# The context mixer's convolution beside the x tokens' second routing pass

## The reference

```python
p  = modulate(rms_norm(h, norm1_g), ...) @ w_in          # q, k, v, pool input, conv input, two conv gates, 3 gates
o  = diff_attn_core(q, k, v, lam)                        # 8 heads, two softmaxes per head
pool = pool_branch(p[pool input], pool_w, pool_scale)
conv = (b_gate * depthwise_conv(c_gate * conv_in, conv_w)) @ conv_out_w      # kernel of 3 tokens
h  = h + gate * ((g0 * attn + g1 * pool + g2 * conv) @ w_out)
# peer_ffn: for each token and 8 heads the best 16 of 128 x 128 experts
s  = einsum(xn2 @ w_q, sub_keys); s1, i1 = top_k(s[0], 16); s2, i2 = top_k(s[1], 16)
top_s, pos = top_k(s1 + s2, 16); eidx = i1 * 128 + i2 at pos; gate = softmax(top_s)
h  = h + m5 * sum_k gate_k * gelu(xn2 . u_emb[eidx_k]) * v_emb[eidx_k]       # 8 x 16 = 128 experts per token
```

## Time and profile before

| | us |
|---|---|
| Time, median of 3 runs (4295.15 to 4298.55) | 4296.83 |
| The profiled execution | 4289.55 |
| Its span | 4287.3 |
| PE busy | 3734.7 (87%) |
| DVE busy | 2834.8 (66%) |
| ACT busy | 1158.1 (27%) |
| POOL busy | 907.4 (21%) |

### The profile page before, as it was taken

How to read it: one execution, slowest core, us unless ns; L and a number is a source line. 1 busy time by engine, 2 the same in 40 slices (tenths; PEclk the granted TensorE clock), 3 DMA queues, 4 the chain that set the end, 5 groups by cost and what they waited for, 6 DMA issues and landing times.

```text
span 4287.3 us, 42560 instructions
## 1 busy us (share of the span) xinstructions
PE 3734.7 (87%) x15389; PEld 2387.8 (56%) x15389; DVE 2834.8 (66%) x6600; ACT 1158.1 (27%) x2577; POOL 907.4 (21%) x772
## 2 busy tenths in 40 slices
PE   7999998788999879987777888777779989999898
PEld 3457554334745535543333554222239879898797
DVE  3241137988877797888785568886656676565764
ACT  2140011124111112122101422111124444444443
POOL 0000013433333343334341024443320000000000
PEclk9999999999999999998898999999999999999999
DMA  6363458988999999999995179999974534455343
GB/s 251 147 256 128 171 195 353 412 346 303 412 420 367 393 394 371 409 378 365 408 421 230 40 313 388 421 383 421 422 306 171 185 129 167 177 176 180 129 167 133
DMA packets 246622, 1225.90 MB, mean 286 GB/s; under 512 B 19256, under 2 KB 46202, under 8 KB 124428
## 3 DMA queue, kind: packets, MB, share of 16 engines
q0 software_dynamic: 110592, 805.36, 46.1%
q1 hardware_dynamic: 135820, 417.84, 26.3%
HBM read 1222.07 MB, written 1.05 MB: 285 GB/s over the span
## 4 chain that ended last, share of the span: by engine, by line
PE 40%; DMA 16%; DVE 15%; ACT 3%; issue 2%; POOL 1%; DVEq 0%; ACTq 0%; SPq 0%; POOLq 0%
PE ps L446 11%; DMA BIG<-in_t_uv,idx 10%; PE ps L795 7%; PE ps L820 7%; PE ps L821 7%; PE ps L822 7%; DMA gbuf<-in_t_uv,idx 4%; DVE BIG L1954 2%; DVE gbuf L1954 2%; DMA wbuf<-in_t_uv,idx 1%; DVE BIG L1947 1%; DVE wbuf L1954 1%; PE ps L434 1%; DVE plo L1995 1%; PE ps L439 1%
## 5 line engine op out<-in xcount | busy, mean ns | idle before, releaser
L446 PE MATMUL ps<-wbuf,BIG 128*128 128x512 f32 x1856 | 824.0, 600 | 7.8 <-ACT BIG L1231 4.4
L2809 POOL DMA_INDIRECT gbuf<-in_t_uv,idx x286 | 336.8, 1178 | 1439.8 <-DVE BIG L1867 835.1
L446 PEld LDWEIGHTS ps<-wbuf,BIG 128*128 128x128 f32 x1856 | 356.0, 193 | 453.9 <-issue 443.9
L1995 DVE TENSOR_TENSOR plo<-wbuf,phi 128x1024 fp32r<-128x1024 f32 (+1 forms) x344 | 401.6, 1180 | 284.5 <-ACT phi L1336 283.8
L795 PE MATMUL ps<-gbuf,BIG 128*128 128x512 f32 x868 | 430.6, 635 | 149.1 <-ACT BIG L1301 149.1
L795 PE MATMUL ps<-BIG 128*128 128x512 f32 x904 | 436.0, 622 | 114.5 <-ACT BIG L1301 114.4
L1316 ACT ACTIVATE BIG<-BIG 128x2 f32<-128x2 f32 x384 | 78.2, 204 | 1445.4 <-DVE BIG L1961 1431.5
L820 PE MATMUL ps<-XH,phi 128*128 128x256 f32 x1472 | 421.6, 286 | 24.6 <-DVE XL L2005 20.7
L1954 DVE CUSTOM_DVE_ANT_0 BIG<-BIG 128x1024 f32<-128x1024 f32 x292 | 355.7, 1221 | 115.6 <-DMA BIG<-in_t_uv,idx 114.8
L1954 DVE CUSTOM_DVE_ANT_0 gbuf<-gbuf,BIG 128x1024 f32<-128x1024 f32 x286 | 348.0, 1221 | 124.3 <-DMA gbuf<-in_t_uv,idx 123.3
L2809 POOL DMA_INDIRECT BIG<-in_t_uv,idx x292 | 342.6, 1173 | 403.3 <-PE ps L795 325.4
(11 more groups left out here) (368 smaller groups left out, 5062.0 us busy)
## 6 DMA issues: line engine op xcount, KB each, us to landing
wbuf<-in_t_in SPq DMA_DIRECT2D x84, 1024.0 KB
wbuf<-in_ffn_wg SPq DMA_DIRECT2D x20, 2048.0 KB, 7.6
wbuf<-in_ffn_wu SPq DMA_DIRECT2D x20, 2048.0 KB, 7.7
wbuf<-in_t_conv SPq DMA_DIRECT2D x48, 768.0 KB
wbuf<-in_t_w_mod SPq DMA_DIRECT2D x32, 1024.0 KB
wbuf<-in_ffn_wd SPq DMA_DIRECT2D x16, 2048.0 KB, 7.9
wbuf<-in_t_peer_wq SPq DMA_DIRECT2D x24, 1024.0 KB
wbuf<-in_w_in SPq DMA_DIRECT2D x14, 1536.0 KB, 6.5
```

Of the source, the lines that this page charges most:

```text
L446: ins = p(mm)(bank, l, r, start=(k == 0), stop=(k == 7))
L1995: v(tt)(lo, W2.of(key, rows_, n)[:, k0:k1, c0:c1], hi.bitcast(F32), ALU.subtract).then_inc(dve_piece.up(q), 1)
L2809: g(nc.gpsimd.indirect_dma_start)(slot, None, I["t_uv"], bass.IndirectOffsetOnAxis(ap=idx[:, tb % 3, j:j + 1], axis=0)).then_inc(g_landed[ ...
```

## The change

The convolution of the context moves from behind the pooled input to beside the routing pass of A 1, on PE, ACT and DVE. The pass goes at 0.5, the convolution at 0.55 with a rate of 0.66, and the remainder of `beside` at 0.72 instead of 0.6. The convolution uses the scratch ring `side_b` (BIG 10240 to 12287) instead of `side4`, and DVE resets that ring on PE's last scores of the pass. SP issues the convolution's tiles ahead of the Q/K tiles. `QT` and `UU` of `beside` move to BIG 18432 (the scores region `SS`), `CV` to BIG 0 (the normalised x tokens, gather buffer 6). So buffer 7 stays with the gathers. ACT's wait for it goes, and SP waits for its last row ahead of layer 1's small rows. The ring has seven buffers up to slot 151, eight for 152 to 219, nine for 220 to 239, then as before. In group A 1 PE adds the v rows of slots 0 to 23 too, and DVE begins its own sum at slot 25.

```diff
-        beside.QT, beside.MM, beside.UU, beside.PL, beside.CV = by_col(24576), by_tok(8192, 2), by_tok(24576, 2), by_col(10240), by_col(24576)
+        beside.QT, beside.MM, beside.UU, beside.PL, beside.CV = by_col(18432), by_tok(8192, 2), by_tok(18432, 2), by_col(10240), by_col(0)
...
-                if n < 2 and T in "BC":
-                    rows_gone(a, {"B": 7, "C": 8}[T])
+                if n < 2 and T == "C":
+                    rows_gone(a, 8)
...
-                        if i == 1:
+                        if i == (25 if T == "A" else 1):
                             v(ts)(ACCB, row, wv[:, i:i + 1], None, ALU.mult).then_inc(dve_exp.up(T, tb, "v", i), 1)
...
-            return (T, tb) not in SHARED or j % 4 == 0 or (T == "A" and j >= 104)
+            return (T, tb) not in SHARED or j % 4 == 0 or (T == "A" and (j < 24 or j >= 104))
...
         def dve_context(v):
             yield from dve_rest(v, "A", 0)
-            yield from scaled(dve_route_pass(v, "A", 0, 1), 0.72, 1)
-            yield from scaled(dve_beside(v), 0.6, 1)
+            route = scaled(dve_route_pass(v, "A", 0, 1), 0.5, 1)
+            yield next(route)
+            yield from alongside(route, scaled(dve_beside_first(v), 0.55, 1), 0.66)
+            yield from scaled(dve_beside(v), 0.72, 1)
             yield 6
             yield from scaled(dve_route_pass(v, "B", 0, 2, 0, 2), 0.6, 1)
+
+        def dve_beside_first(v):
+            v.wait_ge(*pe_peer.at("A", "pq", 3, 3))
+            side_b.reset((pe_route, ("A", 1, 12)))
+            yield from dve_conv(v, "B", 0, beside, side_b)
...
             yield from dve_pooled(v, "B", 0, L)
-            yield from dve_conv(v, "B", 0, L, side4)
             yield from dve_gates(v, "B", 0, L, side4)
...
-                if s == 64:
-                    gat.held, gat.freed[6] = {8, 9}, ((pe_peer, ("A", "pq", 3, 3)),)
-                if s == 90:
-                    gat.held = {7, 8, 9}
-                if s == 140:
-                    gat.held, gat.freed[8] = {7, 9}, ((pe_att, ("B", 3, NH - 1, "s", 1)),)
+                if s == 152:
+                    gat.held, gat.freed[8] = {6, 9}, ((pe_att, ("B", 3, NH - 1, "s", 1)),)
+                if s == 220:
+                    gat.held, gat.freed[6] = {9}, ((pe_mix, ("B", "br", 1, 2, 1)),)
+                if s == 240:
+                    gat.held = {7, 9}
...
+            sync_conv(s, "B", 0)
             sync_qkv(s, "B", 0, 0, range(2))
             sync_pooled(s, "B", 0)
-            sync_conv(s, "B", 0)
...
             after_edge(s, "ahead")
+            rows_gone(s, 7)
             sync_layer_rows(s, 1, sideb.slots[0][:, 0:256])
```

More of the change, by code:

```diff
@@ L2505, in pe_context, with pe_beside_first @@
             yield from pe_rest(p, "A", first.XT)
-            yield from scaled(pe_route_scores(p, "A", "A", 1), 0.72, 1)
-            yield from scaled(pe_beside(p), 0.6, 1)
+            route = scaled(pe_route_scores(p, "A", "A", 1), 0.5, 1)
+            yield next(route)
+            yield from alongside(route, scaled(pe_beside_first(p), 0.55, 1), 0.66)
+            yield from scaled(pe_beside(p), 0.72, 1)
             yield 6
             yield from scaled(pe_route_scores(p, "B", "A", 2, 0, 2), 0.6, 1)
+        def pe_beside_first(p):
+            yield from pe_conv(p, "B", 0, beside)
         def pe_beside(p):
@@ L2518, in pe_beside @@
             yield from pe_pooled(p, "B", 0, L)
-            yield from pe_conv(p, "B", 0, L)
             yield from pe_gates(p, "B", 0, L)
@@ L2610, in act_context, with act_beside_first @@
             yield from act_rest(a, "A")
-            yield from scaled(act_route_pass(a, "A", 1, route_before("A", 1, 0)), 0.72, 1)
-            yield from scaled(act_beside(a), 0.6, 1)
+            route = scaled(act_route_pass(a, "A", 1, route_before("A", 1, 0)), 0.5, 1)
+            yield next(route)
+            yield from alongside(route, scaled(act_beside_first(a), 0.55, 1), 0.66)
+            yield from scaled(act_beside(a), 0.72, 1)
             yield 6
             yield from scaled(act_route_pass(a, "B", 2, route_before("B", 2, 0), 0, 2), 0.6, 1)
+        def act_beside_first(a):
+            yield from act_conv(a, "B", 0, beside, side_b)
         def act_beside(a):
@@ L2623, in act_beside @@
             yield from act_pooled(a, "B", 0, L)
-            yield from act_conv(a, "B", 0, L, side4)
             yield from act_gates(a, "B", 0, L, side4)
```

## The result

| | us |
|---|---|
| Before, median of 20 runs | 4297.34 |
| Changed, median of 20 runs | 4303.77 |
| Forecast | 4283 (4264 to 4300) |
| Ratio, changed to before | 1.0014 (1.0007 to 1.0020) |
| Profiled execution, changed | 4302.12 (span 4300.3) |

What follows compares the result with a forecast made beforehand. The prediction saw no single bound: PE short of work, then DMA, then both full. Terms 203 + 180 + 139 + 55 + 64 + 69 = 710 against 724.0 before, 14 us less: 4296.83 - 14 = 4283, range 4264 to 4300.

Steps and rivals of the forecast that it cites:

- Gates and mixer's end: Two stretches after the pooled input: gates 139 us (before 133.0), mixer's end, norm and rows 55 (before 51.5).
- Pass: A1's routing pass with the convolution beside it: PE binds, 203 us, where the two stretches took 250.0 before.
- My analogue, B's second pass: Same weave with the other convolution, all v rows on PE: 219.8 us, 217.7 busy, 2.1 idle.
- The second rival: In the pass, gathers with seven buffers arrive late while tiles load: pass 233 us, in all 740, +16; chance 0.11.
- Attention and pooled input: Stretch from Q/K products through pooled input: 180 us, bounds 174 and 188, with 9 us idle; before 161.1.
- the first rival: PE's extra 18 rows eat the gain, attention keeps 14 us idle: 725, +1 us; chance 0.27 with the middle cases.
- the prediction's own sign of being wrong: PE idle as before in attention (or above 10 us in the pass behind diagonals while DVE waits for gathers).
- Queries: The context's query stretch after the mixer's end: one more v row on PE, 64 us; DMA 57.
- B's first scores: Last stretch, to the end of A1's experts: one more slot at full DMA, 69 us for 66.3.
- The third rival: Better than forecast: attention without idle (174), gates bound by PE (134), pass 200: 693, -31; chance 0.12, part of faster.
- The edits at nothing: Priced at nothing: buffer counts, buffer 7's wait moved to SP, DVE's queue order, ACT's extra work, SP's tile order.
- The Trainium skill's rule: Each DMA engine takes queues in turn, packet by packet, so a tile under way takes half the rate from gathers.

Runs made afterwards that it cites:

- e3: Changed kernel, but SP loads only an eighth of each of the context's gate, conv-out, w_out and query tiles; 4287.86 us, ratio to before 0.9978.
- e10: Changed kernel with fewer slots beside mixer's end, norm and rows (0.4 for 0.72), more beside gates (0.76) and queries (0.9); 4309.32 us, ratio to before 1.0029.
- e12: Changed kernel with gates, mixer's end, norm and rows at 0.6, queries 0.72, Q/K, attention and pooled input 0.853; 4296.13 us, ratio to before 1.0002.
- e5: Changed kernel with one gather buffer fewer (six) from slot 48 to 151; 4338.32 us, ratio to before 1.0084.
- e9: Changed kernel, but SP loads only a sixth of each tile of the context's convolution; 4298.10 us, ratio to before 1.0005.
- e1: Changed kernel with the old sharing of A1's v rows (every fourth on PE below slot 104); 4310.21 us, ratio to before 1.0033.
- e8: Changed kernel with A1's first 24 v rows half on PE (even slots), half on DVE; 4305.33 us, ratio to before 1.0011.
- e7: Changed kernel with the rest of the context's mixer at 0.6 as before, leftover slots at the weave's end; 4330.99 us, ratio to before 1.0072.

## Why the prediction was wrong

The sum was 710 and became 731.6, so 21.6 us were missing, from four terms.

- **Gates and mixer's end**: 139 + 55 = 194 forecast, 203.6 measured, 9.6 of the 21.6. The failed step is "rows can be gathered up to three slots earlier, in the stretch ahead that has room". The room was there and stayed unused: in the pooled input, ahead of the gates, the DMA share was 0.85, and POOL stood four times for 28.7 us in all until a v row on PE freed a buffer. The gates came out even shorter than said (137), with 4.0 us of PE idle, and the rows owed were paid where PE next needs DVE's queue. So the second failed term is the 7.6 us of chain in the mixer's end, carried over from before, which became 18.5. e3, e10 and e12 show that the two stretches together hang on the rows and slots in the gates: lighter tiles, more slots and fewer slots there change their sum by -11.4, +1.5 and -18.1 us. I also gave the gates five more rows where my own table of slots has six (31 to 37; POOL's count is 32 and 38), 2.5 us of DMA time.
- **Pass**: 203 forecast, 208.3 measured. The mechanism held: PE full (202.2 busy), 24 products spread over it, DMA 0.97. The 199.9 us of work was 2.3 short, and idle was 6 instead of 3, of it one wait of 4.5 us for a diagonal. My analogue, B's second pass, had an eighth buffer for half its length, and e5 shows that buffers count here. The second rival (233 us, tiles starve the gathers) did not come: e9 bounds the tiles at 3 us.
- **Attention and pooled input**: 180 forecast, 184.3 measured. Busy was 171.6 for 171.0 said. Idle was 12.8 instead of 9: the chain stayed nearly as long as before (14.1), as the first rival had it and as the prediction's own sign of being wrong says. That its 18 rows eat the gain was half right. They are 30.9 us of PE's work, but with them on DVE (e1) or half on DVE (e8) the two stretches took 187.8 and 185.2 us.
- **Queries** 63.9 for 64, and **B's first scores** 71.6 for 69: nothing, and 2.6 us. In the scores all of PE's 21.1 us of waiting is for diagonals (L1301); in e1, e3, e5, e8 and e9, with the same slots left for it, the stretch took 67.2 to 70.6 us, so 2.6 us may be this one execution's.

B's first scores start at 1434.3 us, where 1415 was forecast. The mistake behind the first term is that I priced each stretch as the larger of PE's and the DMA engines' need, and let what exceeded it vanish where one stretch ends and the next begins. Of the rivals, the first (+1 us, no change) was nearest: its gates of 145 and end of 56 come to 201, for 203.6 measured. That is luck in part, as its gates were 8 us too long and its end 10.6 too short. The measured change lies within the 0.2% that the prediction gave 0.27. The third rival's sum, 693, takes attention at 171, PE's bare work; with the 174 that it names it is 696. The edits at nothing held: SP issues layer 1's small rows 4.2 us before the end of A1's experts in both kernels (at 1493.47 and 1501.68 us), so its new wait for buffer 7 cost nothing.

The Trainium skill's rule (DMA: Bandwidth & Descriptors, section Queues, rings and completion order), that queues share an engine packet by packet, is neither borne out nor refuted. No run here separates it from a shared total.

## What to carry to other kernels

When work is moved to fill an engine's idle time, also price what takes the place it left: here 20 slots came out of two stretches at 2.1 us each (41.8 us) and went into others at 2.5 us (49.5). Where an engine runs ahead because nothing makes it wait, a debt of the DMA engines isn't gone; look for the next instruction that needs the waiting engine's queue, and put the debt there. Slots moved into a stretch that ends in such a handover are dear, and a scale for each stretch (e12) took the loss away here, though it brought no gain.

## What the runs showed of the hardware

- After PE's wait of 4.76 us at the handover the granted clock was 0.50 to 0.52 for 12 us, in which PE waited another 5.15 us (eight transpose records took 1.94 us for 1.06, sixteen of the products 9.24 for 7.03). After the 2.91 us of waiting ahead of it, eight records still took 1.06.
- The 47 slots of e7's last stretch, most with nothing beside them, took 2.7 us each at a DMA share of 0.95, as those of the routing pass before did (58 slots in 154.2 us). The granted clock averaged 0.71 there, with PE busy 66 of 127.5 us.
- A wait that the profile puts down to "issue" can be another engine's queue: PE's 5.15 us before L446 end 0.1 us after DVE's copy does, in the kernel before as well.
